# Attention values and row sums in column tiles, normalized out of PSUM by VectorE, and one GpSimd wait

## What is computed

```python
def one(qi):
    s = jnp.einsum("bqhd,bkhd->bhqk", qi, k).astype(jnp.float32) * scale
    p = jax.nn.softmax(s, axis=-1).astype(v.dtype)
    return jnp.einsum("bhqk,bkhd->bqhd", p, v)
...
o = _attend(q_full, k_full, v).reshape(B, N, N_HEADS * V_DIM) @ p["w_attn_proj"]
```

## Time and profile before

| what | value |
| --- | --- |
| median of 3 runs | 2763.88 us (2762.38 to 2764.07) |
| the profiled execution | 2761.58 us |
| its span | 2759.8 us |
| mean granted TensorE clock | 0.994 |
| PE busy | 97% of the span |
| weight loads (PEld) | 92% |
| DVE, ACT, POOL | 73%, 44%, 23% |

### The profile page before, as it was taken

One profiled execution on the slowest core, in us unless ns is written; L12 is line 12 of the kernel. 1 busy time (PEld: TensorE's weight loads), 2 busy tenths in 40 slices (PEclk: granted clock), 3 DMA queues, 4 the chain that ended last, 5 costly groups with the idle time before them and its releaser, 6 DMA issues. The chain is left out here.

```text
span 2759.8 us, 44748 instructions
## 1 busy us (share of the span) xinstructions
PE 2689.4 (97%) x17878; PEld 2536.0 (92%) x17878; DVE 2017.3 (73%) x2736; ACT 1216.1 (44%) x1998; POOL 622.6 (23%) x323
## 2 busy tenths in 40 slices
PE   6999999999999999999999999999999999999997
PEld 3999999977799999999989999999778999999997
DVE  6878878766534788887888879787664358776876
ACT  5533435556422543343564335355563236443433
POOL 1322422022100124232321413210220002242230
PEclk9999999999999999999999999999999999999999
DMA  6445432210121253423224444322101222212312
GB/s 239 152 147 161 146 123 68 72 56 26 43 84 63 92 168 116 130 99 109 93 101 152 139 159 145 102 75 67 46 27 64 74 65 85 92 63 84 105 49 77
DMA packets 86446, 273.02 MB, mean 99 GB/s; under 512 B 8736, under 2 KB 10016, under 8 KB 86112
## 3 DMA queue, kind: packets, MB, share of 16 engines
q1 hardware_dynamic: 84800, 265.60, 29.1%
q10 hardware_dynamic: 1440, 4.56, 0.5%
HBM read 267.21 MB, written 2.92 MB: 98 GB/s over the span
## 5 line engine op out<-in xcount | busy, mean ns | idle before, releaser
L624 POOL TENSOR_TENSOR sums_raw<-raw_pairs 128x1024 f32<-128x1024 f32 x88 | 238.3, 2708 | 1627.9 <-DVE weights_lo L1706 1050.2
L652 PE MATMUL ps<-h_hi,weights_hi 128*128 128x322 f32 (+1 forms) x1408 | 440.3, 313 | 8.6 <-DVE t_lo L1706 3.1
L656 PE MATMUL ps<-h_hi,weights_lo 128*128 128x322 f32 (+1 forms) x1408 | 437.4, 311 | 0.0
L654 PE MATMUL ps<-h_lo,weights_hi 128*128 128x322 f32 (+1 forms) x1408 | 436.8, 310 | 0.0
L1706 DVE TENSOR_TENSOR weights_lo<-sums_raw,weights_hi 128x1024 fp32r<-128x1024 f32 (+2 forms) x296 | 329.7, 1114 | 56.5 <-ACT weights_hi L1237 26.7
L652 PE MATMUL ps<-t_hi,weights_hi 128*128 128x322 f32 (+1 forms) x1056 | 332.2, 315 | 5.3 <-DVE h_lo L1706 5.3
L652 PE MATMUL ps<-a_hi,weights_hi 128*128 128x320 f32 x1408 | 325.1, 312 | 3.3 <-DVE tmp L1884 2.5
L656 PE MATMUL ps<-t_hi,weights_lo 128*128 128x322 f32 (+1 forms) x1056 | 327.5, 310 | 0.0
L654 PE MATMUL ps<-t_lo,weights_hi 128*128 128x322 f32 (+1 forms) x1056 | 326.4, 309 | 0.0
L654 PE MATMUL ps<-a_lo,weights_hi 128*128 128x320 f32 x1408 | 321.5, 309 | 0.0
L656 PE MATMUL ps<-a_hi,weights_lo 128*128 128x320 f32 x1408 | 321.5, 309 | 0.0
(11 more groups left out here) (273 smaller groups left out, 5680.6 us busy)
## 6 DMA issues: line engine op xcount, KB each, us to landing
raw_pairs<-in_w_up SPq DMA_DIRECT2D x87, 1024.0 KB, 4.9
wm<-in_w_mod SPq DMA_DIRECT2D x88, 512.0 KB, 3.9
raw<-in_w_merge SPq DMA_DIRECT2D x32, 704.0 KB, 4.0
sums_raw<-in_w_down SPq DMA_DIRECT2D x56, 384.0 KB, 3.2
wm<-in_w_mod SPq DMA_DIRECT2D x80, 256.0 KB, 3.0
sums_raw<-in_w_down SPq DMA_DIRECT2D x64, 320.0 KB, 3.0
raw<-in_w_in SPq DMA_DIRECT2D x16, 512.0 KB, 3.6
raw<-in_w_out SPq DMA_DIRECT2D x16, 512.0 KB, 3.5
```

The source lines that it names most:

```text
L624: nc.gpsimd.tensor_tensor(sums_raw[:, UNIT:3 * UNIT].rearrange("p (s c) -> p s c", s=2), w.rearrange("p (s c) -> p s c", s=2)[:, :, 0:UNIT ...
L652: nc.tensor.matmul(out, whi, v, start=first, stop=False)
L654: nc.tensor.matmul(out, whi, v, start=False, stop=False)
L656: mm = nc.tensor.matmul(out, wlo, v, start=False, stop=last)
```

## The change

The ones half of `vals` is no longer used. For j < 6 a value product becomes two matmuls with 64 stationary columns, one for each half of the 512 queries, into the partitions 0 to 63 and 64 to 127 of bank 7, and four matmuls of 32 columns of ones, one for each quarter of the queries, into the partitions 0, 32, 64 and 96. For j = 6 it becomes one matmul of 64 value columns and one of 64 ones. All results of a head now lie in bank 7. The copies by ACT are gone. DVE takes reciprocals straight from PSUM, after every head, and writes the normalized values to `o32` in nine products. `scores(1)` no longer waits for the head before. Elsewhere, GpSimd's sums of pair 44 also wait for the low part of the last gated tile of F1.

```diff
@@ -342,7 +342,7 @@
         vt = tmp[:, 2 * SAMPLE + 2 * T:2 * SAMPLE + 2 * T + KEYS]
-        sums = acc
+        sums_inv = acc[:, 0:2 * P]
         mod_acc = [tmp[:, g * D:(g + 1) * D] for g in range(2)]
@@ -438,7 +438,7 @@
         s_st, s_exp, s_pv = sem("scores_ready"), sem("exp_ready"), sem("values_mixed")
-        s_o32, s_rinv, s_on = sem("o_copied"), sem("row_inverse"), sem("o_normed")
+        s_o32, s_rinv = sem("o_normed"), sem("row_inverse")
         s_ohi, s_olo = sem("o_hi_ready"), sem("o_ready")
@@ -621,6 +621,8 @@
                     pool.wait_ge(s_lo34, pair)
+                    if pair == 2 * PAIRS:
+                        pool.wait_ge(s_alo, pair + START)
                 nc.gpsimd.tensor_tensor(sums_raw[:, UNIT:3 * UNIT].rearrange("p (s c) -> p s c", s=2),
@@ -1084,10 +1086,8 @@
                         pe.wait_ge(s_exp, t0)
-                    if j == 1:
-                        pe.wait_ge(s_o32, hd)
-                        if h == 0:
-                            pe.wait_ge(s_frlo, (l + 1) * 3)
+                    if j == 1 and h == 0:
+                        pe.wait_ge(s_frlo, (l + 1) * 3)
                     if j >= 2:
@@ -1103,8 +1103,19 @@
                     pe.wait_ge(s_exp, t0 + j + 1)
-                    out, v_in = (bank(7), ex[j % 2]) if j < 6 else (bank(1 if following else 3, 0, P), ex[j % 2][:, 0:P])
-                    nc.tensor.matmul(out, vals[b][:, j, :], v_in, start=j in (0, 6), stop=j in (5, 6)).then_inc(s_pv, 1)
+                    v = vals[b][:, j, b * VD:(b + 1) * VD]
+                    if j < 6:
+                        for n in range(2):
+                            nc.tensor.matmul(bank(7, 0, S2)[n * VD:(n + 1) * VD], v, ex[j % 2][:, n * S2:(n + 1) * S2],
+                                             start=j == 0, stop=False)
+                        for n in range(4):
+                            mm = nc.tensor.matmul(bank(7, S2, S2 + P)[32 * n:32 * n + 32], ones[:, 0:32],
+                                                  ex[j % 2][:, n * P:(n + 1) * P], start=False, stop=j == 5)
+                    else:
+                        nc.tensor.matmul(bank(7, S2 + P, S2 + 2 * P)[0:VD], v, ex[j % 2][:, 0:P], start=True, stop=True)
+                        mm = nc.tensor.matmul(bank(7, S2 + P, S2 + 2 * P)[VD:P], ones[:, 0:VD], ex[j % 2][:, 0:P],
+                                              start=True, stop=True)
+                    mm.then_inc(s_pv, 1)
@@ -1581,18 +1592,8 @@
 
-            def o_copy(hd):
-                s = hd % 2
-                o_rows, s_rows = slice(s * VD, (s + 1) * VD), slice((1 - s) * VD, (2 - s) * VD)
-                act.wait_ge(s_pv, (hd + 1) * 7)
-                act.wait_ge(s_olo, hd // 2)
-                for dst, rows in ((o32, o_rows), (sums, s_rows)):
-                    nc.scalar.activation(two(dst[o_rows]), bank(7)[rows].rearrange("p (a n) -> p a n", a=2), ACT.Copy)
-                    ins = nc.scalar.activation(pro(dst[o_rows]), bank(1 if (hd + 1) % HEADS else 3, 0, P)[rows], ACT.Copy)
-                ins.then_inc(s_o32, 1)
             def o_hi(l, t):
-                act.wait_ge(s_on, l * OT + t + 1)
+                act.wait_ge(s_o32, (l * OT + t + 1) * 2)
                 nc.scalar.activation(ot_hi[:, t, :], o32[:], ACT.Copy).then_inc(s_ohi, 1)
@@ -1625,10 +1626,6 @@
                     maximum_hi(hd + 1)
-                if h == HEADS - 2:
-                    maximum_copy(hd + 1)
-                o_copy(hd)
-                if h < HEADS - 2:
                     maximum_copy(hd + 1)
@@ -2098,9 +2095,6 @@
                 dve.wait_ge(s_out, (l + 1) * 32)
-                for s in range(2):
-                    c = (1 - s) * VD
-                    nc.vector.memset(vals[s][:, :, c:c + VD], 1.0)
                 dve.wait_ge(s_k1hi, l + 1)
@@ -2121,8 +2115,6 @@
                 for h in range(HEADS):
-                    if h and h % 2 == 0:
-                        o_norm(l, h // 2 - 1)
                     weight_lo(c0 + HEADS_C + h + 2)
@@ -2132,7 +2124,7 @@
                         maximum_lo(hd0 + h + 1)
-                o_norm(l, OT - 1)
+                    o_norm(hd0 + h)
                 o_lo(l, OT - 1)
@@ -2207,16 +2199,23 @@
 
-            def o_norm(l, t):
+            def o_norm(hd):
+                rows0 = hd % 2 * VD
+                dve.wait_ge(s_pv, (hd + 1) * 7)
+                nc.vector.reciprocal(sums_inv[:, 0:P], bank(7, S2, S2 + P))
+                nc.vector.reciprocal(sums_inv[VD:P, P:2 * P], bank(7, S2 + P, S2 + 2 * P)[VD:P]).then_inc(s_rinv, 1)
+                dve.wait_ge(s_rinv, hd + 1)
+                for n in range(4):
+                    for r in range(0, VD, 32):
+                        tt(o32[rows0 + r:rows0 + r + 32, TOK[n]:TOK[n] + P],
+                           bank(7, n % 2 * P, (n % 2 + 1) * P)[n // 2 * VD + r:n // 2 * VD + r + 32],
+                           sums_inv[32 * n:32 * n + 32, 0:P], ALU.mult)
+                tt(pro(o32[rows0:rows0 + VD]), bank(7, S2 + P, S2 + 2 * P)[0:VD], sums_inv[VD:P, P:2 * P],
+                   ALU.mult).then_inc(s_o32, 1)
+            def o_lo(l, t):
                 dve.wait_ge(s_o32, (l * OT + t + 1) * 2)
-                for n in range(2):
-                    ins = nc.vector.reciprocal(halves(sums)[n], halves(sums)[n])
-                ins.then_inc(s_rinv, 1)
-                dve.wait_ge(s_rinv, l * OT + t + 1)
-                tt(o32[:], o32[:], sums, ALU.mult).then_inc(s_on, 1)
-            def o_lo(l, t):
-                dve.wait_ge(s_on, l * OT + t + 1)
                 dve.wait_ge(s_ohi, l * OT + t + 1)
```

## The result

| | before | after |
| --- | --- | --- |
| median | 2763.98 us (4 runs, 2762.38 to 2764.36) | 2811.4 us (4 runs, 2808.61 to 2812.83) |
| profiled execution, its span | 2761.58, 2759.8 us | 2808.61, 2806.8 us |
| mean granted TensorE clock | 0.994 | 0.989 |

The account below looks back on a forecast made before the run. The prediction took TensorE, 97% busy, to bound the kernel; 22.8 + 2.4 - 1.6 + 1.3 - 3.0 = +21.9 us gave 2785 against 2763.9, with a range of 2756 to 2806.

Parts of the forecast that it names:

- Part 1, the products: Attention value products on TensorE: 1.09 us each against 0.853, +22.8 us; short products +2.4, going in hidden at heads' starts -1.6.
- The short products: The 16 value products of 128 columns, standing between two changes of tiling: 0.15 us each, +2.4 us, bounds 0 and 0.35.
- The forecast's own sum without any changing over: Rival that changing over is free in the value products: -22.2 us, 2742; chance 0.17.
- Part 2, evacuation: VectorE normalizes each head in about 4.0 us of 4.4 available: hidden at 12 of 14 boundaries, +1.3 us at last heads.
- 9 x 0.21: Nine small normalization products on VectorE at 0.21 us each: 0.29 out of PSUM, less 0.08 of overlap between neighbours.
- upper bound, 4.7 us: VectorE's normalization per head if records did not overlap, costing 0.3 x 12 = 3.6 us.
- Hidden at 12 of 14 boundaries, by 0.4 us: Between heads, VectorE's normalization of about 4.0 us fits in the 4.4 us before TensorE wants bank 7 again.
- 0.7 later, twice: +1.3: Before each layer's last head, VectorE is done at 724.6 against TensorE's arrival at 723.93, so TensorE waits: +1.3 us.
- Part 3, the wait on GpSimd: Holding pair 44's sums until F1's last gated tile removes a TensorE wait and slow clock: -3 us, bounds -3.9 and 0.
- I give 1 us back: Allowance for VectorE updates and splits slowed by the later pair 44 sums: up to -3.9 becomes -3 us.
- The one at 2813: Rival: width changes in value products cost a full 0.35, +24 us, and VectorE's normalization shows, +3.6: 2813; chance 0.08.
- forecast signs: Expected after: products 1.1 us, weight-load idle, attention near 155 us, two waits of about 0.7, full clock around pair 44's sums.

## Why the prediction was too low

The parts, in attention time but for the last two. A head's or a last head's time is counted from its two-column products to the next ones, or to the merge:

| part | forecast | measured | from |
| --- | --- | --- | --- |
| tiled products | +23.6 | +22.9 | 292.3 - 269.3 |
| last head of each layer, wait | +1.3 | +2.7 | 2 x 1.87, less 2 x 0.54 for ACT's copies |
| the slow clock behind it | none | +13.0 | 308.2 - 295.2 |
| the other twelve boundaries | 0 | +3.7 | 12 x 0.31 |
| wait on GpSimd | -3.0 | 0 | the two runs with and without |
| outside the attention | none | +5.2 | 47.4 - 42.2 |
| sum | +21.9 | +47.4 | 47.5 by the rounded parts |

The 5.2 outside are 1.1 ahead of the first attention, 1.6 between the first merge product and layer 1's attention, 2.0 behind the second, by the same starts in the two profiles, and the rest between profile and median. They weren't followed to a cause, except that the merge still begins at a low clock: its first product takes 0.90 us at 754.96, and 0.56 in the kernel without the wait. Since other kernels differ by up to 3.1 us in the same way, without a cause that was looked for, not all of the 5.2 need be the change's.

**Part 1, the products: right.** 1.14 us each instead of 1.09. Going in (0.10) and coming out (0.25) were read off the modulation step in the trace of before and hold here; the change of width, for which no row existed, costs 0.15 instead of 0.10. The short products, put at +2.4, show no price of their own: block 6 follows block 5 with no full-array product between, and shares its way out. To price by the group that shares type and tile count, and not by the two-column products without a gap, was sound. The rule of the Trainium skill ("TensorEngine Tiling (Array Packing)", Key Properties), that a change of tiling mode drains TensorE, holds for these fp32 products, at 0.50 us per product. The span formula of the Trainium skill ("TensorE: Matmul & The Clock Gate", Measured speedup vs the span model) has no such term, and the trace disagrees with it. The forecast's own sum without any changing over was 2742.

**Part 2, evacuation: wrong twice.** The first failure is the "9 x 0.21" with its "Neighbours overlap by 0.08". That overlap was read from two reciprocals in SBUF; operations out of PSUM stand end to end at 0.287. (The terms as written add up to 3.84, which the text rounds to "about 4.0".) The text had this as its upper bound, 4.7 us, and charged it "0.3 x 12 = 3.6"; measured are 4.63 and 3.7. So what was to be "Hidden at 12 of 14 boundaries, by 0.4 us" shows at all of them. The second is the dear one, the last head's "0.7 later, twice: +1.3". The delay itself is 1.3 for each layer, 2.7 in all, because the normalization takes 0.6 longer than the forecast gave it. It makes one idle time of 1.96 us, where one of 0.59 for ACT's copies stood before. The step that the prediction doesn't have at all is **what TensorE does after a 2 us wait**: 13 us of lower clock. Its own rows held the warning: behind a wait of 2.16 us the clock was 0.61 and 0.53, and the text even priced that at 1.7 us, as a gain for part 3. It was not carried over to the wait that the change adds. Even so it would have been too low: the full-array stage there was back at full clock after 3.4 us, the tiled products after 17.

**Part 3, the wait on GpSimd: wrong.** The stall at F1's end did go. "I give 1 us back" for what is late next was too little: 2.1 us came back at once, as a longer wait at F2's first product, and the rest before layer 1's attention.

**The rivals.** The one at 2813 ("width changes cost a full 0.35, and DVE's normalization shows") has the right time for the wrong reason: the normalization does show, at 3.7, but a change of width costs 0.15, and where it put 24 us stand 13 of clock and 5 outside the attention. That the time is near 2813 is luck. No case of the list was the true one: none has a term for the clock. (The forecast's terms, 21.9 on 2763.9, make 2786 and not 2785.)

Of the forecast signs these held: a product's pace, the loads' idle time at three places, the full clock and no wait at F1's end. Others didn't: the attention is 21 us longer per layer, not 12, the waits in the last heads are 1.96 and not 0.7, and of the two signs that would make the forecast wrong one is there, a first value product that waits for DVE at every boundary.

## What to carry to other kernels

Where TensorE is full, price a wait by what stands behind it, and not by its length alone: look for the granted clock in stretches of a few us after each wait of the old trace, and ask what kind of products will follow the new one. A split into column tiles saves columns, but each change between full array and tiles, and between widths, is paid at every alternation; here each one saved 0.21 us of columns and cost 0.50. And an operation that a change moves to PSUM is priced by a row that reads PSUM, its overlap with its neighbours too.

## What the runs showed that I had not expected

- After a wait of 2 us the clock went to 0.50 and stayed there through 17 to 20 us of fully busy work with tiled fp32 products of 64 and 32 columns in it (17 and 10 with 64 alone); with full-array products in the same place it was 3.4 and 6.8. Filling the wait with nine spare products kept it at 1.00.
- The clock's part hung on 1.4 us of VectorE's time: 0.57 of waiting instead of 1.96 left the clock at 1.00, worth 6.5 us of clock for each place.
- A stall removed in one stage gave nothing (1.0001 [0.9992, 1.0009]): 2.1 us of it came back some 45 us later, as 2.93 us of wait instead of 0.87, and nothing was left at layer 1's attention.
- Of the 24 us of changing over that pairing the products takes away, 7.9 came.
- Short waits had no fixed outcome: 0.51 us was followed by a low clock in five heads of 14 of one kernel, 0.60 us in one layer of two of another, the latter with full-array products only.

Open stays what decides that, why tiled products between score products keep the clock low so long (a slow stretch with tiled pairs in it lasted 3.4 us), and what the 5 us outside the attention are. No version that beats the kernel before was found, and every tiled variant that computes everything pays more in changes than it saves in columns.
